# Routing gates of 128 expert blocks: scattered by adding transfers into a DRAM table instead of spread by matmuls, with the activated products kept on chip

## The reference

```python
def _peer(x, wq, subkeys, u_tab, v_tab):
    q = (xf @ wq).reshape(T, PEER_HEADS, 2, PEER_KEY_DIM)
    s = jnp.einsum('thcd,ckd->thck', q, subkeys)
    sv, si = lax.top_k(s, PEER_TOPK)
    cand = (sv[:, :, 0, :, None] + sv[:, :, 1, None, :]).reshape(T, PEER_HEADS, 256)
    cv, ci = lax.top_k(cand, PEER_TOPK)
    ea = take_along_axis(si[:, :, 0], ci // 16); eb = take_along_axis(si[:, :, 1], ci % 16)
    experts = ea * 128 + eb
    gate = softmax(cv)
    act = gelu(einsum('cd,ced->ce', xc, u_tab[experts]))
    y = einsum('ce,ced->cd', act * gate, v_tab[experts])
```

## Time and profile before

| | us |
|---|---|
| median of 3 runs (2879.91 to 2881.44) | 2881.43 |
| span of the profiled execution, first to last instruction | 2873.8 |
| U stage of layer 0, first to last gelu | 418.8 |
| V stage of layer 0 | about 348 |

### The profile page before, as it was taken

One profiled execution on the slowest core, in us unless ns is written; L12 is line 12 of the kernel. 1 busy time (PEld: TensorE's weight loads), 2 busy tenths in 40 slices (PEclk: granted clock), 3 DMA queues, 4 the chain that ended last, 5 costly groups with the idle time before them and its releaser, 6 DMA issues.

```text
span 2873.8 us, 45650 instructions
## 1 busy us (share of the span) xinstructions
PE 2764.3 (96%) x16972; PEld 2429.3 (85%) x16972; DVE 2261.0 (79%) x4363; ACT 1602.6 (56%) x2771; POOL 86.7 (3%) x150
## 2 busy tenths in 40 slices
PE   8898999999999999999999999999999999999998
PEld 5676887977888879999998888887899999988886
DVE  4666888876665668999997888866689999888887
ACT  3433554344554644678894554545457689755453
POOL 1000111010002000000000000020000000000000
PEclk9999999999999999999999999999999999999999
DMA  8433676664556235665558777752466665687775
GB/s 297 146 110 132 257 267 252 236 231 161 184 190 223 95 120 189 200 209 194 194 192 265 242 241 242 231 198 74 142 197 212 201 197 189 203 268 241 242 241 165
DMA packets 211292, 579.73 MB, mean 202 GB/s; under 512 B 24096, under 2 KB 87872, under 8 KB 210048
## 3 DMA queue, kind: packets, MB, share of 16 engines
q1 hardware_dynamic: 161568, 491.00, 51.5%
q0 software_dynamic: 13792, 53.28, 5.5%
q10 hardware_dynamic: 35712, 32.52, 3.3%
HBM read 541.05 MB, written 35.65 MB: 201 GB/s over the span
## 4 chain that ended last, share of the span: by engine, by line
PE 76%; DVE 17%; ACT 4%; issue 1%; DMA 0%; ACTq 0%; DVEq 0%; POOLq 0%
PE psum L758 75%; DVE wr L2155 4%; DVE gmem L2155 4%; DVE oh_r L2152 3%; DVE gmem L2158 2%; ACT gmem L1544 2%; ACT wr L1544 1%; ACT crf L1544 1%; DVE xmem L2158 1%; DVE xr L2155 1%; DVE gmem L3048 1%; DVE xmem L2155 0%; PE psum L839 0%; DVE small L2934 0%; ACT xmem L1544 0%
## 5 line engine op out<-in xcount | busy, mean ns | idle before, releaser
L758 PE MATMUL psum<-xr,wr 128*128 128x256 f32 (+1 forms) x9760 | 1293.3, 293 | 18.6 <-DVE xr L2155 9.2
L2155 DVE TENSOR_TENSOR wr<-raw,wr 128x1024 fp32r<-128x1024 f32 (+1 forms) x814 | 994.4, 1223 | 388.3 <-ACT wr L1544 386.9
L758 PEld LDWEIGHTS psum<-xr,wr 128*128 128x128 f32 x9760 | 1237.0, 192 | 63.8 <-DVE xr L2155 14.7
L1544 ACT ACTIVATE wr<-raw 128x1024 fp32r<-128x1024 f32 x808 | 847.9, 1050 | 278.8 <-PE psum L758 257.9
L758 PE MATMUL psum<-wr,cr 128*128 128x512 f32 x3072 | 697.5, 390 | 5.0 <-DVE cr L2155 5.0
L758 PEld LDWEIGHTS psum<-wr,cr 128*128 128x128 f32 x3072 | 576.6, 188 | 125.4 <-ACT cr L1544 3.3
L1544 ACT ACTIVATE cr<-xmem 128x256 fp32r<-128x256 f32 x256 | 107.2, 419 | 338.7 <-PE psum L758 336.6
L1544 ACT ACTIVATE gmem<-psum 128x512 f32<-128x512 f32 (+2 forms) x303 | 169.1, 570 | 212.6 <-PE psum L758 190.0
L758 PE MATMUL psum<-wr,xr 128*128 128x512 f32 (+1 forms) x960 | 238.6, 402 | 8.2 <-DVE gmem L2155 3.7
L758 PEld LDWEIGHTS psum<-wr,xr 128*128 128x128 f32 x960 | 177.9, 195 | 53.0 <-issue 6.3
L1544 ACT ACTIVATE xmem<-psum 128x256 f32<-128x256 f32 x256 | 97.3, 380 | 195.9 <-PE psum L758 186.9
(11 more groups left out here) (174 smaller groups left out, 1592.2 us busy)
## 6 DMA issues: line engine op xcount, KB each, us to landing
raw<-in_uv SPq DMA_DIRECT2D x512, 512.0 KB, 4.8
raw<-in_ffn_in SPq DMA_DIRECT2D x88, 512.0 KB, 3.8
gs<-xmem ACTq DMA_DIRECT2D x248, 128.0 KB, 3.7
xmem<-gs SPq DMA_DIRECT2D x248, 128.0 KB, 4.4
gmem<-in_ada_w POOLq DMA_DIRECT2D x56, 512.0 KB, 4.8
raw<-in_ffn_out SPq DMA_DIRECT2D x44, 512.0 KB, 4.4
raw<-in_ada_w SPq DMA_DIRECT2D x40, 512.0 KB, 3.8
raw<-in_ret_a SPq DMA_DIRECT2D x32, 512.0 KB, 4.3
```

The lines of the kernel that those rows point to most:

```text
L758: ins = pe.matmul(o, a, b, start=first and i == 0, stop=final and i == len(pairs) - 1, skip_group_check=skip)
L1544: return act.activation(o, a, func, **k)
L2155: return dve.tensor_tensor(o, a, b, op)
```

## The change

- `spread`, its one-hot tiles, its matmuls, its two evictions, and the transposes at the end of `router` go, and so does the DRAM tensor `gs` with its 124 writes and 124 reads of 128 KB in a layer.
- `router` now ends with a table address for each of the 128 picks of a token: key a x 32768 + key b x 256 + token, as uint32 in `spot`, and the gate in `worth`.
- A DRAM table `gts[l]` of 128 x 128 x 256 words is cleared by GpSimd's queue in the mixer: one memset of 4 KB a partition and 32 transfers of 512 KB, two in flight.
- GpSimd issues 256 indirect transfers in a layer, 128 for each half of the tokens. Each takes one column of `worth` (128 words, one a partition) and adds each word at its address in the table. Before every 16th it waits until all before it have landed. So the picks of one head are 16 transfers in a row.
- The gelu tiles of all 128 blocks stay in `gmem` (`gel_of`). The routing's scratch memory lies in its upper half, so that ScalarE waits before block 64 until `spot` of the second half is written and the table is cleared.
- In the V stage SP reads the gates of a block (128 KB) from the table into `grow`, eight slots in `xmem`. The first eight reads stand ahead of the load of the fourth V unit, and they wait until all 256 transfers have landed. `weigh` multiplies the gelu tile by it.
- PACE lays the two routers, without `spread`, over 56 steps, and `router(l, 0)` is done behind step 22, `router(l, 1)` behind step 55 (from zero). The V units run in order.

```diff
-    spread_ = [1.7, 0.75] * 34
-    both = [v for i in range(68) for v in spread_[i:i + 1] + (pick + rest)[i:i + 1]]
-    costs = pick[-4:] + rest + both + spread_
+    costs = pick[-4:] + rest + pick + rest
...
-        while done_ + n < len(costs) and sum(costs[:done_ + n]) < sum(costs) * (e + 1) / (NEXP - 4):
+        while done_ + n < len(costs) and sum(costs[:done_ + n]) < sum(costs) * (e + 1) / 56:
...
         yield from s["router"](l, 0)
-        yield from in_turn(s["spread"](l, 0), s["router"](l, 1))
-        yield from s["spread"](l, 1)
+        yield from s["router"](l, 1)
...
         def peer_u(l, e):
             split()
-            if late:
-                spill(l)
             act.wait_ge(*done())
-            if e >= NGEL:
-                act.wait_ge(*spills(l, e - NGEL))
-            f(gel[e % NGEL], bank(e % 3)[:, 0:256], AF.Gelu_apprx_tanh).then_inc(*X.act.up(("gelu", l, e)))
-            late.append(e)
+            if e == 64:
+                act.wait_ge(*Q.dve["spot", l, 1])
+                for i in range(2):
+                    act.wait_ge(cleared[l][i], 16 * 16)
+            f(gel_of(e), bank(e % 3)[:, 0:256], AF.Gelu_apprx_tanh).then_inc(*X.act.up(("gelu", l, e)))
...
-            tt(gt, gt, bc(rsm[:, 8:16].unsqueeze(2), [P, 8, 16]), ALU.mult).then_inc(*Q.dve.up())
+            tt(worth[:, a, :].rearrange("p (h k) -> p h k", h=8), gt, bc(rsm[:, 8:16].unsqueeze(2), [P, 8, 16]),
+               ALU.mult).then_inc(*Q.dve.up())
+            ts(slot[:, 1, :], slot[:, 1, :], 256.0, token[:, a:a + 1], ALU.mult, ALU.add).then_inc(*Q.dve.up())
             own(Q)
-            ts(slot[:, 1, :], slot[:, 1, :], -1.0, None, ALU.mult).then_inc(*Q.dve.up(("slot", l, a)))
+            stt(spot[:, a, :], slot[:, 0, :], 32768.0, slot[:, 1, :], ALU.mult,
+                ALU.add).then_inc(*Q.dve.up(("spot", l, a)))
...
         def weigh(l, e):
-            if e < 4:
-                dve.wait_ge(*X.act["gelu", l, BACK[e]])
-            else:
-                dve.wait_ge(*reloads(l, e))
-            tt(gel[e % 8], gel[e % 8], gmat[:, :, BACK[e]], ALU.mult).then_inc(*X.dve.up(("w", l, e)))
+            dve.wait_ge(*X.act["gelu", l, e])
+            dve.wait_ge(*gates_in(l, e))
+            tt(grow[e % 8], gel_of(e), grow[e % 8], ALU.mult).then_inc(*X.dve.up(("w", l, e)))
...
+        def gates(l, e):
             if e >= NEXP:
                 return
+            if e == 0:
+                sp.wait_ge(xs_out[l], 16)
+                for a in range(2):
+                    sp.wait_ge(spread_out[l][a], 16 * 128)
             if e >= 8:
                 sp.wait_ge(*X.dve["c", l, e - 8])
+            sp.dma_start(grow[e % 8], gts[l][e * P * T:(e + 1) * P * T].rearrange(
+                "(p t) n -> p (t n)", p=P)).then_inc(gate_in[e % 8], 16)
...
+            pool.wait_ge(*kin_made[l])
+            pool.memset(clear, 0.0).then_inc(*zeroed.up((l, "clear")))
+            pool.wait_ge(*zeroed[l, "clear"])
+            for k in range(32):
+                if k > 1:
+                    pool.wait_ge(cleared[l][k % 2], 16 * (k // 2))
+                load(gts[l].rearrange("(p w) n -> p (w n)", p=P)[:, 1024 * k:1024 * k + 1024], clear, cleared[l][k % 2])
...
+            for a in range(2):
+                pool.wait_ge(*Q.dve["spot", l, a])
+                for k in range(128):
+                    if k and k % 16 == 0:
+                        pool.wait_ge(spread_out[l][a], 16 * k)
+                    pool.indirect_dma_start(gts[l], bass.IndirectOffsetOnAxis(ap=spot[:, a, k:k + 1], axis=0),
+                                            worth[:, a, k:k + 1], None,
+                                            compute_op=ALU.add).then_inc(spread_out[l][a], 16)
             pool.wait_ge(*W.pe[base_v[l] - 1])
```

More of the change, by code:

```diff
@@ L235, in program @@
     xs = nc.dram_tensor("xs", [P, 2048], F32, kind="Internal").ap()
-    gs = nc.dram_tensor("gs", [NEXP, P, 256], F32, kind="Internal").ap()
+    gts = [nc.dram_tensor(f"gt{l}", [NEXP * P * T, 1], F32, kind="Internal").ap() for l in range(2)]
     x = xmem.rearrange("p (a n) -> p a n", a=2)
@@ L313, in program @@
         units += [(dr["uv"][l][e, :, 0:1024], UNIT) for e in range(NEXP)]
-        units += [(dr["uv"][l][e, :, 1024:2048], UNIT) for e in BACK]
+        units += [(dr["uv"][l][e, :, 1024:2048], UNIT) for e in range(NEXP)]
     NU = len(units)
@@ L356, in program @@
     Q = Trio("route", sem)
-    Z = Trio("spread", sem)
-    trios = [W, X, N, C, G, K, A, R, S, L, Q, Z]
+    trios = [W, X, N, C, G, K, A, R, S, L, Q]
     raw_in = [sem(f"raw_in{i}") for i in range(NRAW)]
@@ L367, in program @@
     zeroed, kin_made = Signal(sem("zeroed")), Signal(sem("kin_made"))
-    spilled = [sem(f"spilled{i}") for i in range(8)]
-    back_in = [sem(f"back_in{i}") for i in range(8)]
+    cleared = [[sem(f"cleared{l}{i}") for i in range(2)] for l in range(2)]
+    spread_out = [[sem(f"spread_out{l}{a}") for a in range(2)] for l in range(2)]
+    gate_in = [sem(f"gate_in{i}") for i in range(8)]
     out_sem = sem("out_sem")
@@ L471, in program @@
     nscr = M.get(512)
+    clear = M.get(1024)
     assert M.spans[0][0] <= 32768 - 2048
@@ L491, in program, with gel_of, gates_in @@
     cu3 = ci[:, 0:128].bitcast(U32).rearrange("p (h k) -> p h k", h=8)
[L492 to L505, removed]
+    grow = [xmem[:, i * 256:(i + 1) * 256] for i in range(8)]
+    def gel_of(e):
+        return gel[:, (e + 16) % 64 if e < 64 else e, :]
+    def gates_in(l, e):
+        return gate_in[e % 8], 16 * (16 * l + e // 8 + 1)
     xo = xrf[:, 0:2048].rearrange("p (a n) -> p a n", a=2)
@@ L1468, in router @@
         def router(l, a):
[L1469 to L1493, removed]
+            for _ in range(16 * a + 2 + 8 + 12 + 1 + 1 + 1 + 1):
                 yield
@@ L1535, in tensor_program @@
                "layer_norm": layer_norm, "peer_start": peer_start, "peer_q": peer_q, "scan": scan,
-               "router": router, "spread": spread, "peer_u": peer_u, "peer_turn": peer_turn, "peer_v": peer_v,
+               "router": router, "peer_u": peer_u, "peer_turn": peer_turn, "peer_v": peer_v,
                "peer_end": peer_end})
@@ L3072, in router @@
-            yield
[L3074 to L3086, removed]
-                        tk = slice(128 * a + 4 * i + j, 128 * a + 4 * i + j + 1)
-                        for s_, half in enumerate((gate_hi.bitcast(F32), keep[:, 3, :])):
-                            ts(oh[g][:, j, s_, :], iota, keep[:, 0, tk], half[:, tk], ALU.is_equal,
-                               ALU.mult).then_inc(*Z.dve.up(("oh", l, a, i) if j == 3 and s_ else None))
-                yield
-                if i > 1:
-                    t4 = 128 * a + 4 * (i - 2)
-                    g = 4 + 2 * (i % 2)
-                    dve.wait_ge(*Z.act["g", l, a, i - 2])
-                    d = gmat[:, t4:t4 + 4, :].rearrange("p (b j) e -> p b j e", b=2)
-                    tt(d, d, bank(g, 2).rearrange("p b (j s e) -> p b j s e", j=2, s=2)[:, :, :, 0, :],
-                       ALU.add).then_inc(*Z.dve.up(("g", l, a, i - 2)))
-                yield
@@ L3182, in sync_program @@
                 if j == base_v[l] - 1:
-                    for e in range(4, 8):
-                        reload(l, e)
+                    for e in range(8):
+                        gates(l, e)
                 if base_v[l] < j < base_v[l] + NEXP:
-                    reload(l, j - base_v[l] + 7)
+                    gates(l, j - base_v[l] + 7)
             load()
```

81 lines of the change are left out of this document (17 added, 64 removed).

## The result

| | before | changed | ratio |
|---|---|---|---|
| median, us | 2880.67 (4 runs, 2874.78 to 2881.44) | 3392.34 (4 runs, 3386.37 to 3394.22) | 1.178, 95% interval 1.1763 to 1.1796 |
| span of the profiled execution | 2873.8 | 3392.4 | |
| layer 0, first to last gelu of the U stage | 418.8 | 366.6 | |
| layer 0, last gelu to first V product | 1.4 | 310.2 | |

The change costs 512 us, 256 a layer. The forecast was 2932 with a range up to 3100: the sign was right, the size was off by a factor of ten, and the time lies outside the range.

What follows compares the result with a forecast made beforehand. TensorE and VectorE were taken as both nearly full in the U stage, the scatter as decisive. V starting 22.3 us later plus 3 for the clear: 25.3 a layer, 51 for two; 2925 against the span, 2932 us as median; range 2772 to 3100.

Steps and rivals of the forecast that it cites:

- The U stage: Expert blocks, first to last gelu: without `spread`, 2.88 us a block over 127 steps, 365.8 us, so 53 us shorter a layer.
- The clear: Zeroing the table in the mixer, 32 writes of 512 KB: between 0 and 10 us a layer, 3 taken.
- c: Time of GpSimd's queue for one indirect issue in the scatter: between 0.57 and 1.69 us, the middle, 1.13, taken.
- the sum: Scatter time a layer: 16 batches, each 15 issues and a last landing, 16 x (15 c + L) = 372 us.
- The port: Rival, chance 0.13: indirect issues falling into VectorE's splits wait 0.22 us each, 53 us a layer more, 3038 in all.
- the main case: Scatter ends too late for the V stage, c above 1.02: 2932 us, own range 2887 to 3060, chance 0.35.
- L: Landing of the last transfer in each batch of 16 in the scatter: 4.3 us from below, 6.3 taken.
- The DMA engines: Rival, chance 0.12: three packets a word at 42 ns plus unit loads, 428 us; V 82 us later a layer, 3045.
- Hidden: Rival, chance 0.24: scatter ends before 1466, c under 0.83 (0.94 at L 4.3); the whole 53 us comes, 2781.
- The room of 295 us: Time for the scatter in layer 0, from the first router's end at 1171 to 1466, before the first table read.
- The V stage: Second expert stage, 343 us of TensorE in one piece; table reads and weighing hidden under it, nothing gained or lost.
- dear c: Upper bound of c, 1.69 us an issue: scatter of 506 us, 3200 us in all.

## Why the prediction was right in sign and wrong in size

- **The U stage.** 53 us were forecast, 52.2 measured; 2.88 us a block, 2.887 measured. VectorE's two routers fitted in 56 steps, and TensorE had no wait for them. Right.
- **The clear.** 3 us charged. The query stage of layer 0 starts at 1055.90 instead of 1050.52, but the same 5.4 us already lie between the two traces where a long piece of TensorE's work starts in the mixer, at 905.31 and 899.95, before the clear begins. In layer 1 the way from GpSimd's first mixer load to the subkeys is 148.3 us in both. So it costs nothing, though its transfers were issued until 1008 instead of 1000.
- **The failed step: c, the time of an indirect issue.** "As nothing in the trace is nearer to one end, I take the middle, 1.13." It measured 1.86 from issue to issue with nothing beside it, above even the upper bound of 1.69: 1.25 us fixed, 0.30 for 128 rows (both estimates from the run with 64 rows), and 0.30 between two. 240 x 0.73 = 175 us a layer, or 350 of the 460 us by which the forecast was short. The instruction alone, 1.55, lies under the bound; the 0.30 between two issues, for which the sum had no term, takes it above. And the bound itself was put together from one plain issue and one arithmetic instruction, neither of which does this work; a sum of two unlike rows is not a bound.
- **The port.** The rival with chance 0.13 was true beside the main case, not instead of it, and priced at 53 us a layer: 68 measured. That the two are near is luck. It took a split as 1.13 us, where the earlier trace rows have 1.22; it charged all 240 issues, where only 106 stood beside the stage; and it took issues as falling at random into splits. They don't: a held-up issue ends 1.42 us behind the split and the next starts just behind the next split, so that 0.39 of the issues waiting became 0.85 of them (86 of 101).
- **The landing.** L was 6.3. From the last issue of a batch to the next it is 6.3 us in the mean of the six pauses beside the loads (1215.67 - 1209.55 = 6.1 the first) and 3.3 in the eight of the hole. Of the 16 that the sum has, one doesn't exist: between the two halves the kernel waits only for the second half's addresses, and the next issue follows 1.86 us behind. The mean of all 16 is about 4.3: 16 x 2 = 32 us too dear. So L was right for a core whose loads run, and the sum had no second value for one that stands.
- Together, with 106 issues at 2.33 us instead of 1.55 beside the U stage (83 us, of which 68 went when the split had its second operand in PSUM): 372 + 175 + 83 - 32 = 598 us, against 603. Six pauses of 1.9 to 3.7 us inside batches, for which the profile shows no cause, add 11; 5 of the 83 are also in the landings.
- **The DMA engines** as the bound: refuted for adding transfers. The queue's row from 1180 to 1470 (packets, MB, share of 16 engines) is

```profile
q0 software_dynamic: 14560, 0.06, 13.1%
```

that is 0.131 x 16 x 290 / 14560 = 42 ns a packet, the forecast price, but about one packet a word instead of three, and no U block came late. In the hole the 16 engines were busy for 0.23 of the time.
- **Hidden.** It needed c under 0.83 to 0.94 (295 / 16 less 6.3, by 15, gives 0.81 for the first). The run without transfers shows that its time was right, 2776 against the forecast 2781. The room of 295 us was right too: scatter less SP's wait is 603.3 - 308.9 = 294 us in the changed kernel and 367.6 - 73.1 = 294.5 with half of the transfers.
- **The V stage** was to stay as it was: 345.6 us for its long piece on the chain against 343.0. Without transfers, so without a hole, it is 343.0 again. The clock stood at 0.51 in the hole, the 1.2 GHz level, and at 0.67 in the mean from 1781 to 1800, before it was back at 1.00; that start costs the 2.6 us.

The range ended at 3100, below the 3200 that the prediction's own dear c gave, and below the 3306 of that c together with the port. Even this is under 3392: an upper end for c that no row had shown should have been left open.

## What to carry to other kernels

An adding indirect transfer of single words cost GpSimd nearly the same with 64 rows as with 128 (1.70 and 1.86 us from issue to issue): count the transfers, multiply by 1.9 us (2.9 beside splits like these, two SBUF operands, 1.22 of each 2.88 us), and compare with the time between the moment the addresses are known and the moment the result is needed. Here that was 256 x 1.9 = 486 us into 295. An idle engine (GpSimd at 3%) is no free place for work until the price of one instruction of that kind has been measured. And two rivals that touch the same term are to be added up, not chosen between.

## What was not expected of the hardware

- An adding indirect issue of 128 words took 1.55 us, a writing one 0.97. An issue of 64 adding words took 1.40.
- An issue that starts while a split runs stands until the split ends and then takes what it still has: it ended 1.42 us behind the split with 128 adding words, 1.27 with 64 and 0.84 when it wrote, each 0.13 us less than an issue alone. The split's own time did not change (1.224 to 1.226 us in 66 of them). Where the way from one split to the next is a little shorter than split, rest and pause together (2.88 against 2.95 us), nearly every issue is caught; at 2.80 us, with 64 rows, the step broke, and the mean fell to 1.63 us an issue.
- Taking one operand out of SBUF wasn't enough by itself: the one-operand split of 0.70 us held issues up as well, the one of 1.22 us with its second operand in PSUM didn't.
- Single-word writes to DRAM, up to 16 transfers of 128 under way, starved the rest of the core: TensorE was busy for 43 of 115 us, the DMA share fell to 0.15 and 42 GB/s, and TensorE's idle time has no releaser in the profile ("issue"). Adding transfers of the same words didn't do it, nor did writing ones with at most four under way. Why is open: that TensorE's own instructions came late would fit, but no run here tests it. The writing issues came 1.27 us apart, the adding ones 1.86 or more, and no run has writing ones as slow with 16 under way. It was seen in both layers of one execution.
